# All low parts of the weight chunks on VectorE, none on GpSimd

## The reference

```python
h = rms_norm(x, norm_mix_g)
u = h @ w_in                      # 2048 -> q | k | v | z | x B C | dt, 12352 columns
q, k, v, z, xbc, dt_raw = split(u)
attn = merged dilated windows of softmax(rms(q) @ rms(k).T * scale + bias) @ v   # 16 heads of 128
xbc = silu(conv5(xbc) + conv_b)   # depthwise, over tokens
y = ssd(x, dt, A0, B, C) + flip(ssd(flip(x), flip(dt), A1, flip(B), flip(C))) + x * d_skip  # 8 groups of 4 heads
ssd = rms_norm_per_group(y * silu(z))
x = x + concat(attn, ssd) @ w_out
x = x + relu(rms_norm(x) @ w_up) ** 2 @ w_down      # 2048 -> 8192 -> 2048
```

## Time and profile before

| | us |
|---|---|
| runs, median of 3 | 1662.77 (1662.34 to 1664.15) |
| the profiled execution's span | 1661.6 |
| PE busy in it | 1547.4 (93%) |
| DVE busy | 781.7 (47%) |
| ACT busy | 726.7 (44%) |
| POOL busy | 956.1 (58%) |

### The profile page before, as it was taken

How to read it: one execution, slowest core, us unless ns; L and a number is a source line. 1 busy time by engine, 2 the same in 40 slices (tenths; PEclk the granted TensorE clock), 3 DMA queues, 4 the chain that set the end, 5 groups by cost and what they waited for, 6 DMA issues and landing times.

```text
span 1661.6 us, 26094 instructions
## 1 busy us (share of the span) xinstructions
PE 1547.4 (93%) x9501; PEld 1383.6 (83%) x9501; DVE 781.7 (47%) x1169; ACT 726.7 (44%) x851; POOL 956.1 (58%) x413
## 2 busy tenths in 40 slices
PE   5898778787699999999999999999999999999998
PEld 5797678776577888888888999889988999889987
DVE  5799899889986646464412322111221121112211
ACT  4253445433454455454434444334443444334442
POOL 4364355343454666565566566666666656666664
PEclk9999889888899999999999999999999999999999
DMA  8664545354445656656555665666656665566563
GB/s 254 189 200 143 149 125 166 102 153 154 125 151 152 185 174 174 190 169 230 180 192 179 176 191 183 196 194 183 182 195 189 178 188 189 191 189 179 179 200 103
DMA packets 186335, 291.58 MB, mean 175 GB/s; under 512 B 13533, under 2 KB 67151, under 8 KB 185984
## 3 DMA queue, kind: packets, MB, share of 16 engines
q1 hardware_dynamic: 183748, 285.92, 56.7%
q10 hardware_dynamic: 2492, 4.36, 0.9%
HBM read 288.04 MB, written 5.34 MB: 177 GB/s over the span
## 4 chain that ended last, share of the span: by engine, by line
PE 79%; DVE 12%; issue 7%; DVEq 1%; DMA 1%; ACT 0%; POOL 0%; ACTq 0%
PE psum L1170 78%; DVE mix L795 3%; DVE mix L804 2%; DVE conv L820 1%; DVE conv L824 1%; DVE cbm L835 1%; DMA x_in<-in_x 1%; DVE actT_lo L771 1%; PE psum L1269 0%; PE psum L1289 0%; DVE w_lo L777 0%; DVE dt_p L1026 0%; PE psum L1215 0%; DVE xbc L829 0%; DVEq L795 0%
## 5 line engine op out<-in xcount | busy, mean ns | idle before, releaser
L430 POOL TENSOR_TENSOR w_lo<-raw,w_hi 128x1024 fp32r<-128x1024 f32 x384 | 939.3, 2451 | 675.5 <-ACT w_hi L492 674.6
L492 ACT ACTIVATE w_hi<-raw 128x1024 fp32r<-128x1024 f32 x512 | 540.7, 1059 | 789.9 <-PE psum L1170 789.9
L1170 PE MATMUL psum<-actT_lo,w_hi 128*128 128x256 f32 x1792 | 517.9, 289 | 17.5 <-DVE w_lo L777 12.1
L1170 PE MATMUL psum<-actT_hi,w_lo 128*128 128x256 f32 x1792 | 512.9, 286 | 0.0
L1170 PE MATMUL psum<-actT_hi,w_hi 128*128 128x256 f32 x1792 | 512.3, 286 | 0.0
L1170 PEld LDWEIGHTS psum<-actT_lo,w_hi 128*128 128x128 f32 x1792 | 350.2, 195 | 28.3 <-DVE w_lo L777 12.9
L777 DVE TENSOR_TENSOR w_lo<-raw,w_hi 128x1024 fp32r<-128x1024 f32 x128 | 161.3, 1260 | 440.2 <-ACT w_hi L492 438.1
L1170 PEld LDWEIGHTS psum<-actT_hi,w_lo 128*128 128x128 f32 x1792 | 350.4, 196 | 0.2
L1170 PEld LDWEIGHTS psum<-actT_hi,w_hi 128*128 128x128 f32 x1792 | 350.0, 195 | 0.0
L1170 PE MATMUL psum<-w_hi,hid_lo 128*128 128x512 f32 x512 | 199.2, 389 | 0.0
L1170 PE MATMUL psum<-w_lo,hid_hi 128*128 128x512 f32 x512 | 199.2, 389 | 0.0
(11 more groups left out here) (189 smaller groups left out, 1464.3 us busy)
## 6 DMA issues: line engine op xcount, KB each, us to landing
raw<-in_w_in SPq DMA_DIRECT2D x128, 512.0 KB
raw<-in_w_up SPq DMA_DIRECT2D x128, 512.0 KB
raw<-in_w_down SPq DMA_DIRECT2D x128, 512.0 KB
raw<-in_w_out SPq DMA_DIRECT2D x64, 512.0 KB
raw<-in_w_in SPq DMA_DIRECT2D x64, 256.0 KB
raw<-in_w_in SPq DMA_DIRECT2D x128, 128.0 KB
decay<-decay_rows SPq DMA_DIRECT2D x16, 512.0 KB, 5.7
rel_tiles<-rel_rows ACTq DMA_DIRECT2D x1, 3072.0 KB, 15.0
```

The costliest lines, as they stand in the source:

```text
L430: pool.tensor_tensor(w_lo[i][:, :, :], raw[j][:, :, :], w_hi[i][:, :, :].bitcast(f32), ALU.subtract).then_inc(lo_pool, 1)
L492: act.activation(w_hi[j % RING][:, :, :], raw[j][:, :, :], ACT.Copy).then_inc(hi_ready, 1)
L1170: return pe.matmul(o, lhsT, rhs, start=first, stop=last, **kw)
```

## The change

GpSimd makes no low part any more and DVE all 512. The counting semaphore `lo_pool` goes, and `wait_low` waits for `lo_dve` at 8 U + j + 1. DVE's queue gets the low part of every chunk at the place where so far only those of chunks 3 and 7 stood: in window 0 one behind each `x_low` of the first seven and one at the end, and everywhere else at the head of each slot. Three steps of window 0 are laid out anew: `dt_softplus` comes in three parts at slots 6, 7 and 8, `dt_sums` at 9 and `dt_tokens` at 14; on PE the transposes for it move from slot 12 to 13, and on ACT the store of the decay rows from slot 11 to 12.

```diff
         def wait_low(eng, U, j):
-            if j in DVE_CHUNKS:
-                eng.wait_ge(lo_dve, len(DVE_CHUNKS) * U + DVE_CHUNKS.index(j) + 1)
-            else:
-                eng.wait_ge(lo_pool, len(POOL_CHUNKS) * U + POOL_CHUNKS.index(j) + 1)
+            eng.wait_ge(lo_dve, CH * U + j + 1)
...
-            def low(U, j):
-                i = j % RING
-                pool.wait_ge(hi_ready, CH * U + j + 1)
-                pool.tensor_tensor(w_lo[i][:, :, :], raw[j][:, :, :], w_hi[i][:, :, :].bitcast(f32),
-                                   ALU.subtract).then_inc(lo_pool, 1)
...
             def att_window(a):
-                for s in range(WIN):
-                    r, j = divmod(s, CH)
-                    if j in POOL_CHUNKS:
-                        low(12 + 3 * a + r, j)
-                    if s == 11 + LEAD:
-                        qk_root(2 * a)
-                    if s == 19 + LEAD:
-                        qk_root(2 * a + 1)
+                qk_root(2 * a)
+                qk_root(2 * a + 1)
...
             def low_ahead(U0, s):
                 n, j = divmod(s + LEAD, CH)
-                if j in DVE_CHUNKS:
-                    low(U0 + n, j)
+                low(U0 + n, j)
...
                 if R > 0:
                     x_low(R - 1)
-                if R == 3:
-                    low(0, 3)
+                    low(0, R - 1)
+            x_low(7)
             low(0, 7)
-            x_low(7)
...
                 low_ahead(0, s)
-                if s == 6:
-                    dt_softplus()
-                if s == 8:
+                if 6 <= s < 9:
+                    dt_softplus(s - 5)
+                if s == 9:
                     dt_sums()
-                if s == 13:
+                if s == 14:
                     dt_tokens()
...
             def mlp_quarter(q, start):
                 for s in range(start, 8 * CH):
                     n, j = divmod(s, CH)
-                    if j in DVE_CHUNKS:
-                        low(MLP_U + 8 * q + n, j)
+                    low(MLP_U + 8 * q + n, j)
```

More of the change, by code:

```diff
@@ L44 @@
 X_SPLIT = 1280
-DVE_CHUNKS = (3, 7)
-POOL_CHUNKS = tuple(j for j in range(CH) if j not in DVE_CHUNKS)
 WIN = 3 * CH
@@ L231, in build @@
         raw_in = [sem(f"raw_in{j}") for j in range(CH)]
-        hi_ready, lo_pool, lo_dve, chunk_used = sem("hi_ready"), sem("lo_pool"), sem("lo_dve"), sem("chunk_used")
+        hi_ready, lo_dve, chunk_used = sem("hi_ready"), sem("lo_dve"), sem("chunk_used")
         x_in_s = [sem(f"x_in{t}") for t in range(TT)]
@@ L425, in _ @@
             pool.tensor_tensor(small[:, 4:6], small[:, 2:4], halfneg[:, 0:2], ALU.pow).then_inc(x_rs, 1)
-            def low(U, j):
-                i = j % RING
-                pool.wait_ge(hi_ready, CH * U + j + 1)
-                pool.tensor_tensor(w_lo[i][:, :, :], raw[j][:, :, :], w_hi[i][:, :, :].bitcast(f32),
-                                   ALU.subtract).then_inc(lo_pool, 1)
-            def unit(U):
-                for j in POOL_CHUNKS:
-                    low(U, j)
             def qk_root(n):
@@ L458, in _ @@
                 att_window(a)
-            with pool.Fori(OUT_U, MLP_U + 32) as U:
-                unit(U)
         @block.scalar
@@ L616, in _ @@
                         .then_inc(rel_stored, 16)
-                if s == 11:
+                if s == 12:
                     act.wait_ge(dt_step, 20)
@@ L1012, in then_step, with dt_softplus @@
                 dve.wait_ge(dt_step, step[0])
-            def dt_softplus():
+            def dt_softplus(part):
+                if part == 2:
+                    for k in (15, 13, 11, 9, 7, 5, 3):
+                        then_step(stt_(p, p, 1.0 / k, z2, ALU.add, ALU.mult))
+                    return
+                if part == 3:
+                    then_step(stt_(p, p, 1.0, z, ALU.add, ALU.mult))
+                    then_step(ts_(r, v, 0.0, None, ALU.max))
+                    then_step(stt_(soft_dt, p, 2.0, r, ALU.mult, ALU.add))
+                    then_step(ts_(a_dt, soft_dt, dtcol[:, 4:5], None, ALU.mult))
+                    return
                 dve.wait_ge(dt_done, 1)
@@ L1024, in dt_softplus @@
                 then_step(ts_(p, z2, 1.0 / 17, None, ALU.mult))
-                for k in (15, 13, 11, 9, 7, 5, 3):
-                    then_step(stt_(p, p, 1.0 / k, z2, ALU.add, ALU.mult))
-                then_step(stt_(p, p, 1.0, z, ALU.add, ALU.mult))
-                then_step(ts_(r, v, 0.0, None, ALU.max))
-                then_step(stt_(soft_dt, p, 2.0, r, ALU.mult, ALU.add))
-                then_step(ts_(a_dt, soft_dt, dtcol[:, 4:5], None, ALU.mult))
             def dt_sums():
@@ L1116, in _ @@
             mid_block(3)
-            low(MLP_U, DVE_CHUNKS[0])
+            low(MLP_U, LEAD)
             dve.wait_ge(squared_mid, 8)
@@ L1160, in mlp_quarter @@
                 down_add(MLP_U + 8 * q + 7, 3, q)
-            mlp_quarter(0, DVE_CHUNKS[0] + 1)
+            mlp_quarter(0, LEAD + 1)
             with dve.Fori(1, 4) as q:
@@ L1172, in _, with chunk_by_weights @@
             pe.sem_inc(y_done, PER_GROUP)
-            def chunk_by_weights(U, j, pair, skip=False):
+            def chunk_by_weights(U, j, pair):
                 wait_low(pe, U, j)
@@ L1340, in _ @@
                     dt_unit()
-                if s == 12:
+                if s == 13:
                     pe.wait_ge(rel_copied, 1)
```

## The result

The new kernel takes 1587.9 us (median of 4 runs, 1587.6 to 1588.5), where the old one takes 1663.4 beside it: a ratio of 0.9547, 95% interval 0.9533 to 0.956. The forecast was 1588, from 1568 to 1618. The total came out right, and part of that is luck: a term that was too small and one that was missing cancelled.

A forecast was written before the change was run, and what follows sets the result against it. The prediction took DVE's queue in the four SSD windows as the bound: 66.7 us saved there plus 8 at the start, nothing elsewhere, 74.7 off the 1661.6 span, giving 1588 us as median, range 1568 to 1618.

The forecast's parts named there:

- What the change removes, 128.9 us: Four SSD windows: lengthening of DVE's instructions by GpSimd's low parts, mean less shortest time, times count; 128.9 us goes.
- What it adds, 83.2 us: Four SSD windows: 73 low parts move to DVE at 1.14 us each, 83.2 us.
- The waits at the low parts, taken as gone: Four SSD windows: DVE's 21.0 us of waiting at 24 low parts vanishes, since PE will be in front.
- The lockstep rival: SSD windows: DVE's low parts meet late `w_hi`; 1609 or 1630 us, chance 0.16 shared with failing attention cover.
- The start, 8 us: Before the SSD windows, to 113.4 us: a gain of 8 us, with ends 0 and 13.
- the split: Start: softplus chain cut in three, removing PE's 5.6 us wait for a low part and about 2 of slow clock.
- the one for the first unit: Start, first unit: six more low parts on DVE, 6.8 us, against idle time and shorter blocked instructions.
- The rest costs nothing, while its cover holds: Attention and MLP: DVE's idle time takes the added low parts at no cost; failing attention cover 10 to 20 us.
- what it moves: DVE's queue: low parts head their slots and wait for `w_hi`; mixer steps and ACT's exponentials wait behind them.
- PE waiting for `w_lo` after the mixer: Stages after the SSD mixer: a sign that the forecast is wrong; no size given.
- the slower case: SSD windows: the lengthening of DVE's instructions isn't GpSimd's, so the time is 1725 us; chance 0.04.
- PE as the bound: SSD windows: PE's own time sets their length; at 318 us the gain is 92, time 1562; chance 0.10.

The follow-up runs named there:

- no_low_parts: The old kernel with GpSimd leaving out its subtractions in units 3 to 14, so nobody makes 72 of 96 low parts there; 1558.69 us.
- start_only: The old kernel with only the new kernel's window 0: all its low parts on DVE and the softplus chain in three parts; 1650.08 us.
- mlp_only: The old kernel with DVE making all low parts of the MLP's 32 units and nothing else changed; 1670.10 us.
- late_add: The new kernel with the last down_add of the MLP's first three quarters moved behind the next quarter's fourth low part; 1578.49 us.
- idle_reads: The new kernel with GpSimd doing 54 useless subtractions of two constants in windows 1 to 3; 1696.6 us.
- one_of_eight: The old kernel with DVE making seven of eight low parts in units 3 to 14, GpSimd only chunk 0's of each unit; 1602.94 us.

## Why the prediction was right, point by point

**The bound was read rightly.** DVE's queue set the length of the four windows, and it still does: busy 318.5 of 340.5 us. With most of its extra work gone, PE becomes the bound (no_low_parts).

**What the change removes, 128.9 us: right to about 1 us.** no_low_parts gives DVE 238.9 us busy where the sum had 238.0. Mean less shortest time, times count, was a good estimate because the short time is what every one of these instructions has when GpSimd is silent.

**What it adds, 83.2 us: right to 4.** Over no_low_parts the new kernel's DVE is busy 318.5 - 238.9 = 79.6 us longer, for 71 low parts where 73 were counted. The sum was 343.9 for the windows; measured are 340.5, with DVE busy 318.5 where 321.2 was forecast.

**The waits at the low parts, taken as gone: right in the reason, not quite gone.** The same row as in the earlier trace rows, now:

```profile
L748 DVE TENSOR_TENSOR w_lo<-raw,w_hi 128x1024 fp32r<-128x1024 f32 x95 | 115.5, 1218 | 5.9 <-ACT w_hi L463 3.1 <-issue 2.5
```

21.0 us went down to 5.9, and 5.3 of these are the two turns of the loop, which are no wait for `w_hi` at all. The lockstep rival is out. The turns were in the 21.0 too (2.1 and 2.0), and the forecast took them as gone with the rest. That it met the idle time all the same (22.0 measured, 22.7 forecast) is luck: 5.9 remained where 0 was written, and the other idle time shrank from 22.7 to 16.1 where it was taken as staying.

**The start, 8 us: mis-sized.** 13.9 in the traces, just beyond the forecast's upper end of 13, and 12.7 as start_only. Nearly all of the 8 was put on the split. At that place the sum even fits (5.6 + 2 = 7.6, and the chunk table has 13.9 - 6.1 = 7.8), but by two causes at once: the split alone gives 3.8, the silence without the split most of the whole. The term that failed is the one for the first unit, which was charged 6.8 us for low parts against "its blocked instructions there get shorter as well", without working the latter out. These are DVE's groups up to PE's second unit, before and then after (count, busy us, mean ns):

```profile
L771 DVE TENSOR_TENSOR actT_lo<-xg,actT_hi 128x512 fp32r<-128x512 f32 x8 | 13.8, 1719 | 0.0
...
L741 DVE TENSOR_SCALAR rs_diag<-ident,small 128x128 f32<-128x128 f32 x2 | 2.6, 1314 | 0.4 <-POOL small L425 0.4
```

```profile
L742 DVE TENSOR_TENSOR actT_lo<-xg,actT_hi 128x512 fp32r<-128x512 f32 x8 | 5.5, 683 | 0.0
...
L712 DVE TENSOR_SCALAR rs_diag<-ident,small 128x128 f32<-128x128 f32 x2 | 0.5, 285 | 0.4 <-POOL small L418 0.4
```

The eight low parts of the activations take 5.5 us in place of 13.8, and the diagonal ahead of the first matmul 0.5 in place of 2.6. That is 10.4 us of work for DVE less there, by the same mean-less-shortest reckoning that the forecast used for the windows and left out here. PE begins 3.2 us earlier and the second unit 6.1.

**"The rest costs nothing, while its cover holds": wrong for the MLP, by 8.7 us.** Attention and the output projection held, to 0.1 us. In the MLP the forecast compared amounts (582 us idle, 217 us of work) and looked for trouble inside attention's steps. What failed was the order: the low part is placed at the head of its slot, but behind a step that waits for the end of the quarter before. Under "what it moves" the forecast asked what waits behind a low part, but not, in the MLP, what the low part stands behind. Of its own signs, that PE stays busy all through the MLP did not come true, and PE waiting for `w_lo` after the mixer, which it had named as a sign of being wrong, did, three times. mlp_only shows the loss by itself, and late_add that this one place is the whole of it.

**Sum.** Forecast 66.7 + 8 - 0 = 74.7. Measured 70.1 + 13.9 - 8.7 = 75.3 in the traces. The errors, +3.4, +5.9 and -8.7, cancel to 0.6. Without the MLP's loss the time would have been late_add's 1578.5, 9.5 below the forecast, though inside the range.

**The rivals.** The lengthening is GpSimd's (no_low_parts and idle_reads), so the slower case is out. The Trainium skill's advice that a saturated VectorE may be relieved even by GpSimd (Perfetto Trace Analysis, Optimizing Scalar/DVE Operations) does not hold here, not even for one low part in eight, and the warning that it gives with it, that moving work between these two might not help, does: one_of_eight loses 0.9 us with each subtraction. PE as the bound was priced from 318 us of PE work in the windows. It is 306.4 when PE never stands still, so that rival would have ended 12 us lower than written.

## What to carry to other kernels

When instructions of one shape vary by a factor of three or more on VectorE, put the GpSimd timeline beside them before anything else. If they match, and VectorE is what bounds the stretch, price GpSimd's work by what it takes from VectorE (here 2.0 us for each 2.4 us subtraction that would take VectorE 1.14 itself), and do this for every such stretch of the program, not only the one that looks worst. And when work is given to a queue that is written out in order, list for each stage what stands ahead of it there and waits: an engine that is idle for most of a stage can still be late at its one long wait.

## What the runs showed of the hardware that was not expected

- The price of sharing. On a full VectorE one GpSimd subtraction of 128x1024 cost the program 2.02 us (idle_reads) and 2.0 to 2.1 (one_of_eight), nearly the 2.4 us that it takes itself, though the windows also hold idle time of DVE.
- Fills are not harmless either: three of 962 ns in place of each subtraction cost 26.6 us over the 54 places, 0.16 us each. DVE's busy time grows by 31.4 us there, 31.9 of lengthening in the two `TENSOR_SCALAR` lines alone.
- The turn of the SSD loop leaves VectorE idle for 2.7 and 2.5 us (2.1 and 2.0 at the same places before the change), for which the profile may name an innocent releaser. PE's loop has its turns at the same windows, and in no_low_parts PE is busy through all of them. What in VectorE's loop sets the price stays open.
